# Delta-rule chunks in a four-layer decoder trunk: VectorE's order of work, and the next chunk's spreading placed ahead of the state's write

## Chip, cores and metric

The kernel runs on one core of a Trainium2 chip. The metric is the time of one execution on the device, in microseconds (us), as the median of several runs. A profiled execution gives a trace of every engine beside it.

## What is computed

The whole kernel is one inference step of a four-layer decoder trunk (sparse attention, gated delta rule, RG-LRU, sparse attention, each followed by a convolutional feed-forward layer) for one prompt of 512 tokens and eight sample tokens. The change lies in the second layer's delta rule over the prompt. In the reference it reads, cut to what matters (the reference takes chunks of 64 tokens, the kernel chunks of 128; the result is the same function):

```python
gcum = jnp.cumsum(gc, axis=-1)
decay = jnp.exp(jnp.where(incl, gcum[..., :, None] - gcum[..., None, :], NEG))
kb = kc * bc[..., None]
lower = jnp.einsum('nbhid,nbhjd->nbhij', kb, kc) * decay * strict
A = lower + jnp.eye(C, dtype=jnp.float32)
rhs = jnp.concatenate([vc * bc[..., None], kb * jnp.exp(gcum)[..., None]], axis=-1)
sol = lax.linalg.triangular_solve(A, rhs, left_side=True, lower=True, unit_diagonal=True)
u_base, w_dec = sol[..., :DV], sol[..., DV:]
attn = jnp.einsum('nbhid,nbhjd->nbhij', qc, kc) * decay

def step(S, xs):
    q_i, k_i, ub, wd, at, g_i = xs
    u = ub - jnp.einsum('bhck,bhkv->bhcv', wd, S)
    o = jnp.einsum('bhck,bhkv->bhcv', q_i * jnp.exp(g_i)[..., None], S) + jnp.einsum('bhij,bhjv->bhiv', at, u)
    g_last = g_i[..., -1]
    S = S * jnp.exp(g_last)[..., None, None] + jnp.einsum(
        'bhck,bhcv->bhkv', k_i * jnp.exp(g_last[..., None] - g_i)[..., None], u)
    return S, o
```

## The kernel before

The trunk is a row of stages. Each is a block of its own, in which every engine has its own list of instructions and waits on counters of the others; the engines meet at a stage's end. The stage here is `gdn_chunks` (L1239 to L1515). It takes the 512 prompt tokens in four chunks of 128 (`NCH`, `CH`), eight heads of width 128, in two groups of four heads (`x` = 0, 1), everything in float32. Queries, keys and values lie in SBUF as feature by token, put there by the stage before; no weights are loaded, and the only DMA is the final state's write at the end (L1511).

The order of the work is written out by hand: for each engine one loop over chunks, in it a list of steps. Every step raises its engine's counter of its group by one (`then_inc`), and `after(engine, who, x, step, c)` waits until `who` has done that step of chunk `c` for group `x`; with `None` for the step it waits for everything of the chunk before. The names of the steps stand in `pe_steps`, `act_steps` and `dve_steps` (L1246 to L1253). PSUM's eight banks are four for each group, numbers 0 to 3.

One chunk goes as follows:

- Spreading (TensorE, `products`, L1294): `spread_g` and `spread_b` copy each head's row of accumulated log decay and of beta to all 128 partitions. Then the products `qk` (queries by keys) and `kk` (keys by `k_beta`, L1328 and L1329).
- ScalarE makes `exp_g` and, from VectorE's `decay` differences (L1446), their exponential.
- VectorE makes `k_beta`, `v_beta`, `q_exp`, `k_exp`, `attn`, and the matrix `lower_t`, in two parts by partitions (L1458 and the line behind it), masked by `strict`. All VectorE operations through the helper `tt` carry line L1430, and most of ScalarE's carry L1393.
- The inversion of the triangular matrix. TensorE turns `lower_t` (`turn_l`, matmuls with the identity, L1313 and L1336), ScalarE copies it to `lower` (L1405). On blocks of 16, three rounds square `power` and `power_t` and grow the inverse `inv_t` (L1306); VectorE adds each growth to `inv_t`. Then three joins (`pair`, `turn`, `join`) take the blocks from 16 to 32, 64 and 128, with `mask0` and `mask1` made by VectorE ahead of the first; the result is `full_t`.
- TensorE turns `v_beta` (`turn_v`, L1299), applies the state (`k_state`), VectorE subtracts (`rhs`), TensorE solves, ScalarE copies `u`. Then for each group `out` (L1383, L1384) and `update`, the product of `k_left` and `u`.
- VectorE copies the output to `v.y` (L1500, seen in the trace as `all_xn_t_sb`), scales the state by its last decay (`decay_s`) and adds `update` (`add_s`).

At the head of a chunk TensorE waits for all of the chunk before:

```python
after(pe, "dve", x, None, c)
after(pe, "act", x, None, c)
```

## Time and profile before

| | us |
|---|---|
| median of 3 runs | 3374.48 |
| lowest and highest | 3372.79, 3377.38 |
| the profiled execution's own time | 3377.42 |
| its span in the trace | 3375.8 |
| mean granted TensorE clock | 0.954 of full |
| stage of the chunks in the trace | about 1134 to 1331 |

The span is the time from the first instruction to the last in the trace, which the profiled execution's own time exceeds by 1.6 us. Times in the rows are microseconds from the span's start. PE is TensorE's matmuls and PEld its weight loads, DVE is VectorE, ACT is ScalarE. A float32 matmul shows as two records where it is a product, and as one where it is a transpose (L1299). The clock is a share of 2.4 GHz, so 0.50 is 1.2 GHz.

### The profile page before, as it was taken

What the parts mean: (1) busy time and instruction counts of PE and PEld (TensorE: products, weight loads), DVE (VectorE), ACT (ScalarE), POOL (GpSimd) and SP (SyncE); (2) the same over time, 40 slices, a digit from 0 to 9 for tenths busy, and PEclk for the clock granted to TensorE, in tenths of its full rate; (3) what the DMA queues carried; (4) which work ended last, traced back from release to release, by engine and by line L of the source; (5) the groups of instructions that cost most, each with busy time, mean ns of one, the idle gap of its engine ahead of it and who ended that gap; (6) DMA issues with size and microseconds to landing.
All of it is one profiled execution on the core that took longest, in us unless ns stands there. A gap on an engine that the chain in (4) does not pass through costs nothing. (4 is left out here: it accounts for less than half of the span.)

```text
span 3375.8 us, 73291 instructions
## 1 busy us (share of the span) xinstructions
PE 3055.0 (90%) x30538; PEld 2845.3 (84%) x30538; DVE 1840.4 (55%) x3293; ACT 1281.6 (38%) x2267; POOL 80.5 (2%) x142
## 2 busy tenths in 40 slices
PE   5988889999899788689999888999979889989998
PEld 5975579999899778479999888999979855889997
DVE  3346646646567554456546565654633456566364
ACT  2236534324255322124233493433322255444242
POOL 0002100000000000000000000000000021000000
PEclk9989999999999898689999998999989999999999
DMA  6635314222322001214222322322265453142322
GB/s 189 200 110 167 113 32 168 81 94 74 87 82 82 6 2 58 81 62 150 88 99 73 98 76 70 142 83 100 80 138 190 145 162 109 32 143 90 110 78 78
DMA packets 154543, 339.44 MB, mean 101 GB/s; under 512 B 58884, under 2 KB 93316, under 8 KB 141332
## 3 DMA queue, kind: packets, MB, share of 16 engines
q1 hardware_dynamic: 145300, 296.04, 27.5%
q0 software_dynamic: 7424, 37.76, 3.2%
q8 instruction: 211, 3.46, 0.4%
q10 hardware_dynamic: 1536, 1.60, 0.2%
q14 instruction: 72, 0.59, 0.1%
HBM read 318.40 MB, written 32.12 MB: 104 GB/s over the span
## 5 line engine op out<-in xcount | busy, mean ns | idle before, releaser
L471 PE MATMUL ffn_ps<-ffn_x_hi_sb,ffn_w_hi_sb 128*128 128x260 f32 x2816 | 571.3, 284 | 49.0 <-DVE ffn_w_lo_sb L592 45.8
L471 PE MATMUL ffn_ps<-ffn_x_hi_sb,ffn_w_lo_sb 128*128 128x260 f32 x2816 | 570.3, 284 | 0.0
L471 PE MATMUL ffn_ps<-ffn_x_lo_sb,ffn_w_hi_sb 128*128 128x260 f32 x2816 | 569.9, 284 | 0.0
L471 PEld LDWEIGHTS ffn_ps<-ffn_x_hi_sb,ffn_w_hi_sb 128*128 128x128 f32 x2816 | 437.7, 190 | 51.4 <-DVE ffn_w_lo_sb L592 47.5
L471 PEld LDWEIGHTS ffn_ps<-ffn_x_hi_sb,ffn_w_lo_sb 128*128 128x128 f32 x2816 | 437.3, 190 | 0.0
L471 PEld LDWEIGHTS ffn_ps<-ffn_x_lo_sb,ffn_w_hi_sb 128*128 128x128 f32 x2816 | 436.7, 190 | 0.0
L526 ACT ACTIVATE ffn_w_hi_sb<-ffn_raw_sb 128x2048 fp32r<-128x2048 f32 (+2 forms) x148 | 249.4, 1685 | 338.5 <-PE ffn_ps L471 338.5
L549 ACT ACTIVATE ffn_pre_sb<-ffn_ps 128x520 f32<-128x520 f32 x176 | 106.6, 606 | 600.7 <-PE ffn_ps L471 312.8
L586 DVE TENSOR_TENSOR ffn_w_lo_sb<-ffn_raw_sb,ffn_w_hi_sb 128x2048 fp32r<-128x2048 f32 (+2 forms) x148 | 296.1, 2001 | 44.9 <-ACT ffn_w_hi_sb L526 44.9
L607 DVE SCALAR_TENSOR_TENSOR ffn_conv_sb<-ffn_pre_sb,ffn_conv_w_sb,ffn_conv_sb 128x512 f32<-128x512 f32 x176 | 132.3, 752 | 340.8 <-ACT ffn_conv_sb L551 340.8
L471 PE MATMUL ffn_ps<-ffn_inner_hi_sb,ffn_w_hi_sb 128*128 128x260 f32 x1408 | 284.7, 283 | 6.5 <-DVE ffn_inner_lo_sb L625 3.4
L471 PE MATMUL ffn_ps<-ffn_inner_lo_sb,ffn_w_hi_sb 128*128 128x260 f32 x1408 | 283.8, 283 | 0.0
L471 PE MATMUL ffn_ps<-ffn_inner_hi_sb,ffn_w_lo_sb 128*128 128x260 f32 x1408 | 282.9, 282 | 0.0
L471 PEld LDWEIGHTS ffn_ps<-ffn_inner_hi_sb,ffn_w_hi_sb 128*128 128x128 f32 x1408 | 217.1, 188 | 9.2 <-DVE ffn_w_lo_sb L586 4.8
L471 PEld LDWEIGHTS ffn_ps<-ffn_inner_hi_sb,ffn_w_lo_sb 128*128 128x128 f32 x1408 | 216.9, 188 | 0.0
L471 PEld LDWEIGHTS ffn_ps<-ffn_inner_lo_sb,ffn_w_hi_sb 128*128 128x128 f32 x1408 | 216.7, 188 | 0.0
L645 DVE TENSOR_TENSOR all_x_t_sb<-all_x_t_sb,ffn_ps 128x520 f32<-128x520 f32 x64 | 44.5, 696 | 268.1 <-PE ffn_ps L471 268.1
L2716 DVE TENSOR_REDUCE nsat_nmax_sb<-nsat_ps 128x2 f32<-128x256 f32 (+3 forms) x128 | 104.9, 821 | 125.0 <-PE nsat_ps L2493 124.9
L201 PE MATMUL nsab_ps<-nsab_x_hi_sb,nsab_w_hi_sb 128*128 128x260 f32 x512 | 114.0, 305 | 43.9 <-DVE nsab_w_lo_sb L291 22.7
L2504 PE MATMUL nsat_ps<-all_consts_sb,nsat_prob_sb 128*128 128x128 f32 x640 | 109.5, 290 | 45.4 <-DVE nsat_prob_t_sb L2741 23.9
L2644 ACT ACTIVATE nsat_prob_t_sb<-nsat_ps 128x128 f32<-128x128 f32 (+3 forms) x192 | 82.2, 437 | 160.0 <-PE nsat_ps L2504 159.8
L2635 ACT ACTIVATE nsat_prob_sb<-nsat_ps,nsat_nmax_sb 128x128 f32<-128x128 f32 (+3 forms) x256 | 132.7, 525 | 25.9 <-DVE nsat_nmax_sb L2716 24.2
(484 smaller groups left out, 5798.7 us busy)
## 6 DMA issues: line engine op xcount, KB each, us to landing
ffn_raw_sb<-ffn_w_in SPq DMA_DIRECT2D x84, 1024.0 KB, 4.8
ffn_raw_sb<-ffn_w_out SPq DMA_DIRECT2D x32, 768.0 KB, 4.2
nsa_ring_sb<-sel_pages SPq DMA_DIRECT2D x160, 128.0 KB, 2.5
ffn_raw_sb<-ffn_w_out SPq DMA_DIRECT2D x32, 640.0 KB, 4.0
...
```

The source lines that it names most:

```text
L201: mm = pe.matmul(out(h), w, x[:, h * H:(h + 1) * H], start=start and k == 0, stop=stop and k == 2)
L471: mm = pe.matmul(psf[:, bank + h, 0:H], wp[:, w[0], w[1]:w[1] + P], xp[:, h * H:(h + 1) * H], start=start and k == 0, stop=stop and k == 2)
L526: act.activation(w_hi[:, s, 0:size], raw[:, s, 0:size], ACT.Copy).then_inc(hi_done, 1)
L549: act.activation(pre[:, s, vg, 2:2 + N].rearrange("p (h n) -> p h n", h=2), src, ACT.Copy)
L586: dve.tensor_tensor(w_lo[:, s, 0:size], raw[:, s, 0:size], w_hi[:, s, 0:size], ALU.subtract).then_inc(lo_done, 1)
L607: own.did(dve.scalar_tensor_tensor(y[:, 0:T], x[:, 1:1 + T], w[1], y[:, 0:T], ALU.mult, ALU.add))
L645: dve.tensor_tensor(x, x, psf[:, 2 * (m % 3):2 * (m % 3) + 2, 0:H], ALU.add).then_inc(added, 1)
L2504: mm = pe.transpose(ps[:, 4 + g2, kt * P:(kt + 1) * P], prob[:, s % 4, g2, kt * P:(kt + 1) * P], g.ident)
L2635: act.activation(prob[:, s % 4, g2, 0:(i + 1) * P], ps[:, 2 * (s % 2) + g2, 0:(i + 1) * P], ACT.Exp, bias=nmax[:, s % 4, g2:g2 + 1], accum ...
L2644: act.activation(prob_t[:, s % 4, g2, 0:(i + 1) * P], ps[:, 4 + g2, 0:(i + 1) * P], ACT.Copy).then_inc(copied[g2], 1)
L2716: dve.tensor_reduce(nmax[:, s % 4, :], ps[:, 2 * (s % 2):2 * (s % 2) + 2, 0:(i + 1) * P], AX, ALU.max, negate=True).then_inc(maxed, 1)
```

## The change

Four things, all inside `gdn_chunks`:

1. VectorE's order. After `k_beta` and `decay` of both groups come `lower_t` and `strict` group by group, then `power_t` and `inv_t`, then `v_beta` and `power`, and the masks directly behind. `q_exp`, `k_exp` and `attn` stand behind the first, second and third pair of adds to `inv_t`.
2. TensorE's order. `kk` follows the spreading, `qk` stands behind `turn_l` and waits for ScalarE's `lower` of its group (its PSUM bank is the turning's). The banks are dealt anew: `spread_b` in 2, `kk` in 1, `qk` in 0. `pair0` waits for the third add (`grown2`), since the masks are earlier.
3. The head of a chunk. TensorE waits for `k_left` and `u` of the chunk before, no longer for all of it, so the spreading may run ahead of `decay_s` and `add_s`. ScalarE's `exp_g` waits for `decay_s`, which still reads the old one.
4. The output's copy to `v.y` goes from VectorE to ScalarE (`store_o`), as its last step in a chunk; the turning of the next chunk's `lower_t`, which writes the same bank, waits for it.

The diff, cut to these:

```diff
@@ TensorE
                 for x in range(2):
-                    after(pe, "dve", x, None, c)
-                    after(pe, "act", x, None, c)
+                    if c:
+                        after(pe, "dve", x, "k_left", c - 1)
+                        after(pe, "act", x, "u", c - 1)
                     products(x, 0, lambda j: v.spread[:, 4 * x + j, :], lambda j: v.rows[:, cols])
-                    products(x, 1, lambda j: v.spread[:, GH + 4 * x + j, :], lambda j: v.rows[:, cols])
-                for x in range(2):
-                    products(x, 3, lambda j: v.k[:, 4 * x + j, cols], lambda j: v.q[:, 4 * x + j, cols])
+                    products(x, 2, lambda j: v.spread[:, GH + 4 * x + j, :], lambda j: v.rows[:, cols])
                 for x in range(2):
                     after(pe, "dve", x, "k_beta", c)
...
                 for x in range(2):
                     after(pe, "dve", x, "strict", c)
+                    if c:
+                        after(pe, "act", x, "store_o", c - 1)
                     half_turns(x, 0, buf["lower_t"], (low, high))
...
+                for x in range(2):
+                    after(pe, "act", x, "lower", c)
+                    products(x, 0, lambda j: v.k[:, 4 * x + j, cols], lambda j: v.q[:, 4 * x + j, cols])
...
-                        after(pe, "dve", x, "masks" if m == 0 else "joined0", c)
+                        after(pe, "dve", x, "grown2" if m == 0 else "joined0", c)
...
                 for x in range(2):
+                    after(pe, "dve", x, "attn", c)
                     turns(x, 0, lambda j: buf["v_beta"][:, x, j, :])
@@ ScalarE
                 for x in range(2):
-                    after(act, "dve", x, None, c)
+                    if c:
+                        after(act, "dve", x, "decay_s", c - 1)
                     after(act, "pe", x, "spread_g", c)
                     run(x, buf["exp_g"][:, x], ps[:, x, 0], ACT.Exp)
...
+                for x in range(2):
+                    after(act, "pe", x, "out", c)
+                    run(x, chunk(v.y, x, c), ps[:, x, 3])
@@ VectorE
                     after(dve, "pe", x, "spread_b", c)
-                    tt(x, buf["k_beta"][:, x], chunk(v.k, x, c), ps[:, x, 1])
-                    tt(x, buf["v_beta"][:, x], chunk(v.v, x, c), ps[:, x, 1])
+                    tt(x, buf["k_beta"][:, x], chunk(v.k, x, c), ps[:, x, 2])
...
                 for x in range(2):
-                    tt(x, buf["q_exp"][:, x], chunk(v.q, x, c), buf["exp_g"][:, x])
-                    after(dve, "dve", x, "k_beta", c)
-                    tt(x, buf["k_exp"][:, x], buf["k_beta"][:, x], buf["exp_g"][:, x])
-                for x in range(2):
                     after(dve, "act", x, "exp_decay", c)
-                    after(dve, "pe", x, "qk", c)
-                    tt(x, buf["attn"][:, x], ps[:, x, 3], buf["decay"][:, x])
                     after(dve, "pe", x, "kk", c)
...
                 for x in range(2):
+                    tt(x, buf["v_beta"][:, x], chunk(v.v, x, c), ps[:, x, 2])
                     after(dve, "act", x, "lower", c)
...
                 for e in range(3):
                     for x in range(2):
                         after(dve, "pe", x, f"grow{e}", c)
                         tt(x, buf["inv_t"][:, x], buf["inv_t"][:, x], ps[:, x, 1, :, low], ALU.add)
...
+                    for x in range(2):
+                        if e == 0:
+                            tt(x, buf["q_exp"][:, x], chunk(v.q, x, c), buf["exp_g"][:, x])
+                        elif e == 1:
+                            tt(x, buf["k_exp"][:, x], buf["k_beta"][:, x], buf["exp_g"][:, x])
+                        else:
+                            after(dve, "pe", x, "qk", c)
+                            tt(x, buf["attn"][:, x], ps[:, x, 0], buf["decay"][:, x])
...
                     after(dve, "pe", x, "out", c)
-                    dve.tensor_copy(chunk(v.y, x, c), ps[:, x, 3]).then_inc(dve_did[x], 1)
                     tt(x, state[:, x], state[:, x], wide(buf["exp_g"][:, x, :, CH - 1:CH]))
```

How the instructions stand at three places of the second chunk. The first is VectorE, from its second `decay` on (`x2` is two such instructions, one for each group of heads). Before:

```order
L1430 TENSOR_TENSOR gdnc_q_exp_sb<-gdn_q_sb,gdnc_exp_g_sb 128x512
L1430 TENSOR_TENSOR gdnc_k_exp_sb<-gdnc_k_beta_sb,gdnc_exp_g_sb 128x512
L1430 TENSOR_TENSOR gdnc_q_exp_sb<-gdn_q_sb,gdnc_exp_g_sb 128x512
L1430 TENSOR_TENSOR gdnc_k_exp_sb<-gdnc_k_beta_sb,gdnc_exp_g_sb 128x512
L1430 TENSOR_TENSOR gdnc_attn_sb<-gdnc_ps,gdnc_decay_sb 128x512
L1458 TENSOR_TENSOR gdnc_lower_t_sb<-gdnc_ps,gdnc_decay_sb 64x4x64
L1430 TENSOR_TENSOR gdnc_lower_t_sb<-gdnc_ps,gdnc_decay_sb 64x512
L1430 TENSOR_TENSOR gdnc_attn_sb<-gdnc_ps,gdnc_decay_sb 128x512
L1458 TENSOR_TENSOR gdnc_lower_t_sb<-gdnc_ps,gdnc_decay_sb 64x4x64
L1430 TENSOR_TENSOR gdnc_lower_t_sb<-gdnc_ps,gdnc_decay_sb 64x512
L1430 TENSOR_TENSOR gdnc_lower_t_sb<-gdnc_lower_t_sb,gdnc_strict_t_packed_sb 128x4x64 x2
L1465 SCALAR_TENSOR_TENSOR gdnc_power_t_sb<-gdnc_lower_t_sb,gdnc_same_packed_sb 128x256 x2
```

Now, from the first `decay`:

```order
L1453 SCALAR_TENSOR_TENSOR gdnc_decay_sb<-gdnc_ps,gdn_cum_tok_sb,all_consts_sb 128x128 x4
L1438 TENSOR_TENSOR gdnc_k_beta_sb<-gdn_k_sb,gdnc_ps 128x512
L1453 SCALAR_TENSOR_TENSOR gdnc_decay_sb<-gdnc_ps,gdn_cum_tok_sb,all_consts_sb 128x128 x4
L1459 TENSOR_TENSOR gdnc_lower_t_sb<-gdnc_ps,gdnc_decay_sb 64x4x64
L1438 TENSOR_TENSOR gdnc_lower_t_sb<-gdnc_ps,gdnc_decay_sb 64x512
L1438 TENSOR_TENSOR gdnc_lower_t_sb<-gdnc_lower_t_sb,gdnc_strict_t_packed_sb 128x4x64
L1459 TENSOR_TENSOR gdnc_lower_t_sb<-gdnc_ps,gdnc_decay_sb 64x4x64
L1438 TENSOR_TENSOR gdnc_lower_t_sb<-gdnc_ps,gdnc_decay_sb 64x512
L1438 TENSOR_TENSOR gdnc_lower_t_sb<-gdnc_lower_t_sb,gdnc_strict_t_packed_sb 128x4x64
L1465 SCALAR_TENSOR_TENSOR gdnc_power_t_sb<-gdnc_lower_t_sb,gdnc_same_packed_sb 128x256 x2
L1438 TENSOR_TENSOR gdnc_inv_t_sb<-gdnc_power_t_sb,gdnc_ident_packed_sb 128x256 x2
L1438 TENSOR_TENSOR gdnc_v_beta_sb<-gdn_v_sb,gdnc_ps 128x512
```

The five wide rows of 128x512 ahead of `lower_t`, and the one between its parts, are gone; `strict` (the rows that read `strict_t_packed`) stands at the end of each group's three, and the first `v_beta` behind `inv_t`.

The second place is VectorE in the rounds of the inversion. Before, from `power` to the masks' first rows:

```order
L1472 SCALAR_TENSOR_TENSOR gdnc_power_sb<-gdnc_lower_sb,gdnc_same_packed_sb 128x256 x2
L1430 TENSOR_TENSOR gdnc_inv_t_sb<-gdnc_inv_t_sb,gdnc_ps 128x256 x6
L1479 TENSOR_TENSOR gdnc_mask_sb<-gdnc_lower_sb,gdnc_pair_packed_sb 128x256
L1430 TENSOR_TENSOR gdnc_mask_sb<-gdnc_lower_sb,gdnc_pair_packed_sb 128x256
L1479 TENSOR_TENSOR gdnc_mask_sb<-gdnc_lower_sb,gdnc_pair_packed_sb 128x256
```

Now, from the last mask to the first join:

```order
L1438 TENSOR_TENSOR gdnc_mask_sb<-gdnc_lower_sb,gdnc_pair_packed_sb 128x256
L1438 TENSOR_TENSOR gdnc_inv_t_sb<-gdnc_inv_t_sb,gdnc_ps 128x256 x2
L1438 TENSOR_TENSOR gdnc_q_exp_sb<-gdn_q_sb,gdnc_exp_g_sb 128x512 x2
L1438 TENSOR_TENSOR gdnc_inv_t_sb<-gdnc_inv_t_sb,gdnc_ps 128x256 x2
L1438 TENSOR_TENSOR gdnc_k_exp_sb<-gdnc_k_beta_sb,gdnc_exp_g_sb 128x512 x2
L1438 TENSOR_TENSOR gdnc_inv_t_sb<-gdnc_inv_t_sb,gdnc_ps 128x256 x2
L1438 TENSOR_TENSOR gdnc_attn_sb<-gdnc_ps,gdnc_decay_sb 128x512 x2
L1438 TENSOR_TENSOR gdnc_inv_t_sb<-gdnc_inv_t_sb,gdnc_ps 128x256 x2
```

The six adds stood together, with the masks behind; now the masks come first, and `q_exp`, `k_exp` and `attn` stand behind a pair of adds each.

The third place is TensorE, from the spreading on (in the first chunk, as in all). Before:

```order
L1294 MATMUL gdnc_ps<-gdn_rows_sb,gdn_spread_sb 128x128 x16
L1294 MATMUL gdnc_ps<-gdn_q_sb,gdn_k_sb 128x128 x8
L1328 MATMUL gdnc_ps<-gdnc_k_beta_sb,gdn_k_sb 64x128
L1329 MATMUL gdnc_ps<-gdnc_k_beta_sb,gdn_k_sb 64x64
L1328 MATMUL gdnc_ps<-gdnc_k_beta_sb,gdn_k_sb 64x128
```

Now, from the last product of `kk` to the first squarings:

```order
L1327 MATMUL gdnc_ps<-gdnc_k_beta_sb,gdn_k_sb 64x64
L1312 MATMUL gdnc_ps<-all_consts_sb,gdnc_lower_t_sb 64x64 x8
L1336 MATMUL gdnc_ps<-all_consts_sb,gdnc_lower_t_sb 64x64 x4
L1312 MATMUL gdnc_ps<-all_consts_sb,gdnc_lower_t_sb 64x64 x8
L1336 MATMUL gdnc_ps<-all_consts_sb,gdnc_lower_t_sb 64x64 x4
L1293 MATMUL gdnc_ps<-gdn_q_sb,gdn_k_sb 128x128 x8
L1305 MATMUL gdnc_ps<-gdnc_power_sb,gdnc_power_t_sb 64x64 x8
L1305 MATMUL gdnc_ps<-gdnc_power_t_sb,gdnc_power_sb 64x64 x8
```

The eight products of queries by keys stood between spreading and `kk`; now they stand behind the turning of `lower_t` and directly ahead of the first squaring.

## Rows read from the trace of the kernel before

**Rows 1.** The page: busy time, share of the span and instructions of each engine
```profile
PE 3055.0 (90%) x30538; PEld 2845.3 (84%) x30538; DVE 1840.4 (55%) x3293; ACT 1281.6 (38%) x2267; POOL 80.5 (2%) x142
```

**Rows 2.** Windows, second chunk: us, busy us (instructions) per engine, PEclk, DMA share, GB/s
```profile
1183.00:1233.00 50.00, 41.63 (x735) 39.72 (x735) 27.57 (x59) 14.17 (x34) 0.00 (x0) 0.93 0.01 2
```

**Rows 3.** Timeline, PE, second chunk: start, us, engine, line, x records [idle before <-releaser]
```profile
1185.85 3.84 PE L1294 MATMUL gdnc_ps<-gdn_rows_sb,gdn_spread_sb 128*128 128x128 f32 x32 [1.09 <-DVE gdnc_state_sb L1430]
1189.53 1.95 PE L1294 MATMUL gdnc_ps<-gdn_q_sb,gdn_k_sb 128*128 128x128 f32 x16
...
1198.79 0.80 PE L1313 MATMUL gdnc_ps<-all_consts_sb,gdnc_lower_t_sb 64*64 64x64 f32 x10 [5.43 <-DVE gdnc_lower_t_sb L1430]
...
1201.72 1.12 PE L1306 MATMUL gdnc_ps<-gdnc_power_sb,gdnc_power_t_sb 64*64 64x64 f32 x16 [0.34 <-DVE gdnc_power_sb L1472]
...
1206.40 0.63 PE L1306 MATMUL gdnc_ps<-gdnc_power_sb,gdnc_power_t_sb 64*64 64x64 f32 x16
...
1209.43 1.10 PE L1306 MATMUL gdnc_ps<-gdnc_power_sb,gdnc_power_t_sb 64*64 64x64 f32 x32
...
1212.89 0.68 PE L1306 MATMUL gdnc_ps<-gdnc_inv_t_sb,gdnc_mask_sb 64*64 64x64 f32 x16 [1.20 <-DVE gdnc_mask_sb L1430]
...
1232.22 1.06 PE L1294 MATMUL gdnc_ps<-gdnc_u_sb,gdnc_k_left_sb 128*128 128x128 f32 x8
1234.36 1.83 PE L1294 MATMUL gdnc_ps<-gdn_rows_sb,gdn_spread_sb 128*128 128x128 f32 x14 [1.09 <-DVE gdnc_state_sb L1430]
```

**Rows 4.** Timeline, DVE, second chunk, same columns
```profile
1187.94 0.69 DVE L1430 TENSOR_TENSOR gdnc_k_beta_sb<-gdn_k_sb,gdnc_ps 128x512 f32<-128x512 f32 x1 [1.55 <-PE gdnc_ps L1294]
...
1191.37 1.12 DVE L1446 SCALAR_TENSOR_TENSOR gdnc_decay_sb<-gdnc_ps,gdn_cum_tok_sb,all_consts_sb 128x128 f32<-128x128 f32 x4
1192.41 0.68 DVE L1430 TENSOR_TENSOR gdnc_q_exp_sb<-gdn_q_sb,gdnc_exp_g_sb 128x512 f32<-128x512 f32 x1
...
1195.53 0.43 DVE L1458 TENSOR_TENSOR gdnc_lower_t_sb<-gdnc_ps,gdnc_decay_sb 64x256 f32<-64x256 f32 x1
1195.97 0.68 DVE L1430 TENSOR_TENSOR gdnc_lower_t_sb<-gdnc_ps,gdnc_decay_sb 64x512 f32<-64x512 f32 x1
...
1198.33 0.74 DVE L1430 TENSOR_TENSOR gdnc_lower_t_sb<-gdnc_lower_t_sb,gdnc_strict_t_packed_sb 128x256 f32<-128x256 f32 x2
1199.00 0.75 DVE L1465 SCALAR_TENSOR_TENSOR gdnc_power_t_sb<-gdnc_lower_t_sb,gdnc_same_packed_sb 128x256 f32<-128x256 f32 x2
...
1201.24 0.43 DVE L1472 SCALAR_TENSOR_TENSOR gdnc_power_sb<-gdnc_lower_sb,gdnc_same_packed_sb 128x256 f32<-128x256 f32 x1 [0.82 <-ACT gdnc_lower_sb L1393]
...
1208.94 0.42 DVE L1430 TENSOR_TENSOR gdnc_inv_t_sb<-gdnc_inv_t_sb,gdnc_ps 128x256 f32<-128x256 f32 x1 [1.91 <-PE gdnc_ps L1306]
...
1211.27 0.89 DVE L1430 TENSOR_TENSOR gdnc_inv_t_sb<-gdnc_inv_t_sb,gdnc_ps 128x256 f32<-128x256 f32 x2 [1.21 <-PE gdnc_ps L1306]
```

**Rows 5.** Timeline, ACT, second chunk
```profile
1187.11 0.60 ACT L1393 ACTIVATE gdnc_exp_g_sb<-gdnc_ps 128x512 f32<-128x512 f32 x1 [7.51 <-PE gdnc_ps L1294]
...
1200.43 0.38 ACT L1405 ACTIVATE gdnc_lower_sb<-gdnc_ps 128x256 f32<-128x256 f32 x1 [7.28 <-PE gdnc_ps L1336]
```

**Rows 6.** Windows of 0.5 us, PE: us, busy (instructions), PEclk, DMA share, GB/s
```profile
1198.50:1199.00 0.50, 0.21 (x4) 0.61 0.00 0
...
1205.00:1205.50 0.50, 0.50 (x16) 0.56 0.00 0
```

**Rows 7.** Timeline, PE, first chunk
```profile
1134.67 6.64 PE L1294 MATMUL gdnc_ps<-gdn_rows_sb,gdn_spread_sb 128*128 128x128 f32 x32 [6.07 <-DVE gdnc_state_sb L1436]
...
1149.97 0.80 PE L1313 MATMUL gdnc_ps<-all_consts_sb,gdnc_lower_t_sb 64*64 64x64 f32 x10 [4.98 <-DVE gdnc_lower_t_sb L1430]
...
1152.90 1.12 PE L1306 MATMUL gdnc_ps<-gdnc_power_sb,gdnc_power_t_sb 64*64 64x64 f32 x16 [0.34 <-DVE gdnc_power_sb L1472]
...
1157.89 0.63 PE L1306 MATMUL gdnc_ps<-gdnc_power_sb,gdnc_power_t_sb 64*64 64x64 f32 x16
```

**Rows 8.** Timeline, DVE, first chunk: its second k_beta
```profile
1141.35 0.69 DVE L1430 TENSOR_TENSOR gdnc_k_beta_sb<-gdn_k_sb,gdnc_ps 128x512 f32<-128x512 f32 x1 [0.47 <-PE gdnc_ps L1294]
```

More of the change, by code:

```diff
@@ L1249, in gdn_chunks @@
     act_steps = ["exp_g", "exp_decay", "lower", "power0", "power_t0", "power1", "power_t1", "power2", "paired0", "inv0",
[L1250 to L1253 removed]
+                 "paired1", "inv1", "paired2", "inv2", "v_tok", "u", "store_o"]
+    dve_steps = ["k_beta", "decay", "lower_t", "strict", "power_t", "inv_t", "v_beta", "power", "masks", "grown0", "q_exp",
+                 "grown1", "k_exp", "grown2", "attn", "joined0", "joined1", "joined2", "rhs", "k_left", "decay_s", "add_s"]
     with ExitStack() as ctx:
```

21 lines of the change are left out of this document (8 added, 13 removed).

## Prediction, made before the changed kernel was run

> **What bounds the kernel now.** A difference under 0.2% (some 7 us) can't be told from no change in a measurement of this kernel, so the question is what the 200 us of the delta-rule chunks can give. I read four views. The page first [rows 1]: over the whole span TensorE is busy 90% and VectorE 55%, which says matmuls bound the kernel; but that is an average over stages of which this change touches one. The windows over that stage next [rows 2]: in a chunk of about 48.5 us (spreading starts at 1185.85 and again at 1234.36) TensorE is busy 41.6 of 50 us, at a mean clock of 0.93. Then the timeline of TensorE in the second chunk [rows 3], for the places where it stands still: 5.43 us before the turning of `lower_t`, 1.20 before `pair0`, 1.09 before the next chunk's spreading. Last the timelines of VectorE and ScalarE beside it [rows 4, 5], for what it waits on.
>
> The largest wait is VectorE's. From the first `k_beta` at 1187.94 it works without a pause past the second `inv_t` at about 1200.4; what the matrix needs of that (`k_beta`, `decay`, `lower_t`, `strict`) is mixed with `v_beta`, `q_exp`, `k_exp` and `attn`, eight wide operations at 0.6 us each (the five from 1192.41 to 1195.53 take 3.12) [rows 4]. TensorE has finished its products at 1193.36 (1198.79 less 5.43) and waits for `strict`. And it pays twice: its granted clock falls from full (2.4 GHz) to half (1.2 GHz) at the end of that wait and comes back in the half microsecond after 1205 [rows 6]. So the first squaring round goes at half: it lasts from 1201.72 to 1206.40, 4.68 us, where the same instructions in the second round, 1206.40 to 1209.43, need 3.03 [rows 3].
>
> **The change, part by part.** Times below are from the start of a chunk's spreading (1185.85 in the second), at full clock.
>
> *Triangular matrix first.* The spreading ends at 3.84 [rows 3]. `k_beta` of the first half of the heads starts at 2.09 as before and its `decay` at 2.70. The second `k_beta` waits for the spreading: 3.88. Its `decay` follows at 4.49 and takes 1.04 (1192.41 less 1191.37), to 5.53. Now `lower_t` comes at once: 5.60, its second part 0.44 later (1195.53 to 1195.97), 6.04. `strict` of the same half must wait for it, 0.71 more: 6.75. In the rows TensorE starts 0.46 after `strict` (1198.33 to 1198.79), so the turning starts at **7.21 in place of 12.94**. The products `kk`, now ahead of `qk`, need 1.95 from 3.84 on and are done at 5.8, before that. The other half's `strict` is 1.50 later (0.35 + 0.44 + 0.71), its turning at 8.71.
>
> *What then ends last.* `power` is made by VectorE after two `power_t`, two `inv_t` (0.34 each) and the first `v_beta` (0.60): 8.25 + 0.33 + 1.34 + 0.60 = 10.5; with 0.48 from VectorE's start to TensorE's (1201.24 to 1201.72) the squaring could start at 11.0. But TensorE has `qk` ahead of it, and half of that now waits for ScalarE's `lower` of the second half: turning issued from 8.71, 24 of the 64-column records at 0.032 us (96 in 3.03), 0.25 to land, 0.81 for the two copies (1200.43 to 1201.24), so 10.5; its 16 records, half of 32 in 3.68 us, take 0.92. Squaring starts at **11.4 in place of 15.87**: 4.47 us less, in three chunks 13.4. In the first chunk the clock is at half during the spreading, which takes 6.64 [rows 7], and stays so: second `k_beta` 1141.35 [rows 8], `strict` 2.87 later, turning at 1144.68, squaring 4.19 after that, 1148.87 in place of 1152.90: 4.0.
>
> *The clock.* The one wait of over 5 us is cut to about 1.4 us (5.8 to 7.2), then come bursts with gaps of 0.8 us or less. The waits of 1.09 and 1.20 us are followed by no fall: a mean clock of 0.93 over 50 us is what the one stretch of 6.8 us at half makes by itself (0.5 x 6.8 / 50 = 0.07) [rows 2, 3]. The change's own is not in the trace: it is longer than these, and the stretch after it is thin. The ends are no fall (the round saves 1.65 us in three chunks and 1.96 in the first, 4.99 less 3.03 [rows 7]) and a fall in every chunk (saves nothing, and turning and `qk` at half cost 0.5 + 1.8 us more). I stand near the first, since 1.4 is nearer to 1.2 than to 5.4, but take off a third of one fall, 0.3 x (1.65 + 2.3) = 1.2 us. Sum here: 4.95 + 1.96 - 1.2 = 5.7.
>
> *Masks before the adds.* `pair0` waits for `mask` today; then it waits for the third add, 1211.27 + 0.48 = 1211.75 in place of 1212.89: 1.14 in each of four chunks, 4.6. The masks go to VectorE's wait for the first `grow`.
>
> *Wide operations in gaps.* Two at 0.60 go behind each pair of adds. What covers them are VectorE's waits for TensorE: 1.91 us before the second round's adds, 1.21 before the third's [rows 4]. `q_exp` fits in the one, `k_exp`, 1.2 us, just into the other: cost 0 to 0.1. `attn`, 1.2 us, takes the place in which the four masks stand now, 1.3 us (0.34 each). I cost all three at nothing; without cover it would be up to 0.6 x 6 us a chunk.
>
> *Spreading ahead of the state's write.* TensorE no longer waits for `add_s`, but for `k_left` and `u`, both long done. `update` is issued at 1232.22 and takes 0.9: spreading from 1233.12 in place of 1234.36, 1.24 us at three joints, 3.7. The next `k_beta` comes 2.09 later, when VectorE has finished both `add_s` (half a microsecond before), so the gain arrives.
>
> *Copy of the result to ScalarE.* On VectorE an operation of 128x512 takes 0.69 us, 0.6 to the next [rows 4]; on ScalarE an operation of that shape takes 0.60 [rows 5] and its next task is `exp_g`, 1.26 us after the spreading starts: free. The copy held `decay_s` and `add_s` behind it, which counts only at the stage's end, 0.6. The added waits of the turning and of `exp_g` for ScalarE's copy or for `decay_s` are over before they are reached. No DMA moves.
>
> Sum: 13.4 + 4.0 + 5.7 + 4.6 + 3.7 + 0.6 = **32 us** of the profiled execution's 3377.4, so 3345.4. That execution lies at the top of the three runs; their median is 3374.5, and against it the forecast is **3342.5 us**.
>
> **The rivals.** *The clock falls all the same.* For it: between 5.8 and 8.7 TensorE has only one burst of 0.7 us. Then the 5.7 us of the clock's sum are gone, and turning and `qk` at half cost up to 2.3 us in each of four chunks: 32 - 5.7 - 9.2 = 17, **3357**. Against it: such bursts follow at less than a microsecond. The Trainium skill's page "TensorE: Matmul & The Clock Gate", Part 4, states that transposes in transpose mode do not count as activity for the clock; by that rule, were it to hold for the turning of `lower_t`, the stretch would look idle until `qk` and this rival would be the case. In this trace the turnings of `lower_t` are plain matmuls with the identity.
>
> *VectorE sets the pace inside the inversion.* If the wide operations are not covered, each of six delays an add by up to 0.6 us: 14.4 in four chunks, **3357** too. Against it: the waits in rows 4 are as long as what is put there.
>
> *Slower.* TensorE never gets back to full clock, since the chunk now has many gaps and no long dense stretch ahead of the squaring. Rows 3 and 7 give the price: spreading takes 6.64 us at half in place of 3.84; with 41.6 busy us a chunk, nearly all at full today, that is some 30 us a chunk, less 33 in all: **about 3460**. It is level with today where some 80 us of the stage more than now go at half (each microsecond at half loses 1 - 3.84/6.64 = 0.42). Against it: in the second half of the chunk, which doesn't change, the clock came back in every chunk.
>
> *It does not do what it says.* If the engines' waits kept the old order in effect, nothing would move, **3374**. The order of instructions shows the new one on both engines.
>
> **How the numbers follow.** Forecast 0.76; clock 0.12; VectorE 0.07; no effect 0.03; slower 0.02. The range goes down to 3336 (no fall, the first of the runs of before 1.7 us under their median, a little more at the joints) and up to 3354, which takes in one or two falls, half-covered wide operations, and the better part of both middle rivals. Faster by over 0.2% are the first three, 0.95; within it 0.03; slower 0.02.
>
> **What the profile after would show.** Right: a wait before the turning of about 1.4 us, and 7.2 us from spreading to turning; squaring at 11.4; PEclk near 1.00 in the second to fourth chunk; `pair0` behind an `inv_t` add, not a mask; chunks of about 39.7 us; spreading directly behind `update`. Wrong would be: PEclk at half around the first round; VectorE without a pause between the rounds and TensorE waiting for adds; a new wait of over 2 us anywhere on TensorE.

## The result and the profile after

| | before | after |
|---|---|---|
| median of 4 runs each, us | 3374.65 | **3348.05** |
| lowest and highest | 3372.79, 3377.38 | 3346.9, 3351.53 |
| ratio, with its 95% interval | | 0.9922 (0.9908 to 0.9937) |
| profiled execution's own time | 3377.42 | 3347.42 |
| span in the trace | 3375.8 | 3345.8 |
| stage of the chunks: first spreading to next stage's first matmul | 200.13 | 174.86 |

The change is faster by 26.6 us of medians; 32 were forecast. The time lies inside the range (3336 to 3354), 5.5 us over the forecast.

The page after, line for line with [rows 1]: TensorE's busy time is lower by 5 us while the span is lower by 30, so what went is mostly waiting of TensorE.

```profile
PE 3049.6 (91%) x30538; PEld 2843.0 (85%) x30538; DVE 1836.0 (55%) x3285; ACT 1285.7 (38%) x2275; POOL 80.3 (2%) x142
```

The windows of after, one for each chunk from its first spreading to the next one's, the last to its `update` (columns as in [rows 2]):

```profile
1132.71:1177.38 44.67, 42.10 (x720) 40.18 (x721) 24.69 (x55) 15.25 (x36) 0.00 (x0) 0.90 0.01 2
1177.38:1219.17 41.79, 39.22 (x722) 37.25 (x721) 25.88 (x58) 15.36 (x36) 0.00 (x0) 0.96 0.01 2
1219.17:1259.53 40.36, 37.79 (x723) 35.87 (x721) 25.89 (x58) 15.36 (x36) 0.00 (x0) 1.00 0.01 3
1259.53:1302.00 42.47, 39.89 (x716) 37.82 (x715) 25.19 (x55) 14.76 (x35) 0.00 (x0) 0.92 0.01 3
```

The second and third chunk hold the same instructions, but take 41.79 and 40.36 us. The seventh number of the line, PEclk, says why: 0.96 in the one, 1.00 in the other, 0.92 in the fourth. The clock was to be near 1.00 in all three.

TensorE's timeline after, second chunk, answers to [rows 3]:

```profile
1177.38 3.74 PE L1293 MATMUL gdnc_ps<-gdn_rows_sb,gdn_spread_sb 128*128 128x128 f32 x32
...
1184.55 0.51 PE L1312 MATMUL gdnc_ps<-all_consts_sb,gdnc_lower_t_sb 64*64 64x64 f32 x10 [1.54 <-DVE gdnc_lower_t_sb L1438]
...
1186.16 0.80 PE L1312 MATMUL gdnc_ps<-all_consts_sb,gdnc_lower_t_sb 64*64 64x64 f32 x10 [0.64 <-DVE gdnc_lower_t_sb L1438]
...
1187.69 2.90 PE L1293 MATMUL gdnc_ps<-gdn_q_sb,gdn_k_sb 128*128 128x128 f32 x16
1190.52 0.68 PE L1305 MATMUL gdnc_ps<-gdnc_power_sb,gdnc_power_t_sb 64*64 64x64 f32 x16
...
1193.60 0.63 PE L1305 MATMUL gdnc_ps<-gdnc_power_sb,gdnc_power_t_sb 64*64 64x64 f32 x16
...
1198.95 0.68 PE L1305 MATMUL gdnc_ps<-gdnc_inv_t_sb,gdnc_mask_sb 64*64 64x64 f32 x16
```

The spreading has no wait in brackets any more. The wait of 5.43 us is now 1.54 with a second one of 0.64, and the turning starts at 7.17 (1184.55 less 1177.38). `pair0` at the end has no wait either, and the first round lasts 3.08 us (1190.52 to 1193.60) where it lasted 4.68. But the second half's turning reads 0.80 for its ten records, not 0.51, and `qk` 2.90. The third chunk has both at full clock:

```profile
1226.34 0.51 PE L1312 MATMUL gdnc_ps<-all_consts_sb,gdnc_lower_t_sb 64*64 64x64 f32 x10 [1.54 <-DVE gdnc_lower_t_sb L1438]
...
1227.96 0.51 PE L1312 MATMUL gdnc_ps<-all_consts_sb,gdnc_lower_t_sb 64*64 64x64 f32 x10 [0.64 <-DVE gdnc_lower_t_sb L1438]
...
1228.86 2.09 PE L1293 MATMUL gdnc_ps<-gdn_q_sb,gdn_k_sb 128*128 128x128 f32 x16
1230.88 0.68 PE L1305 MATMUL gdnc_ps<-gdnc_power_sb,gdnc_power_t_sb 64*64 64x64 f32 x16
```

There the squaring starts at 11.71 (1230.88 less 1219.17), in the second at 13.14. Half-microsecond windows of the second chunk, TensorE alone (us, busy and instructions, PEclk), show the fall as [rows 6] do for before:

```profile
1185.50:1186.00 0.50, 0.02 (x1) 1.00 0.00 0
1186.00:1186.50 0.50, 0.34 (x6) 0.58 0.00 0
...
1189.00:1189.50 0.50, 0.50 (x4) 0.51 0.00 0
1189.50:1190.00 0.50, 0.50 (x7) 1.00 0.00 0
```

The clock drops to half (1.2 GHz) at about 1186.1, at the end of the second wait, and is back by 1189.5, before the squaring. All chunks side by side, in us from each chunk's first spreading:

| | turning | squaring | second round | `pair0` | chunk |
|---|---|---|---|---|---|
| before, chunks 1, 2, 3, 4 | 15.30, 12.94, 12.95, 12.94 | 18.23, 15.87, 15.87, 15.88 | 23.22, 20.55, 20.30, 20.08 | 29.71, 27.04, 26.79, 26.57 | 51.18, 48.51, 48.26, 52.18 |
| after, chunks 1, 2, 3, 4 | 9.92, 7.17, 7.17, 7.16 | 16.02, 13.14, 11.71, 14.02 | 19.10, 16.22, 14.78, 17.67 | 24.45, 21.57, 20.14, 23.02 | 44.67, 41.79, 40.36, 48.04 |

(The fourth runs to the next stage's first matmul.) Three of four chunks had a fall between the turning and the squaring, and chunk 3 had none.

VectorE's timeline after, same chunk, for the operations that were moved into gaps [rows 4]:

```profile
1194.15 1.29 DVE L1438 TENSOR_TENSOR gdnc_q_exp_sb<-gdn_q_sb,gdnc_exp_g_sb 128x512 f32<-128x512 f32 x2
1196.15 0.42 DVE L1438 TENSOR_TENSOR gdnc_inv_t_sb<-gdnc_inv_t_sb,gdnc_ps 128x256 f32<-128x256 f32 x1 [0.71 <-PE gdnc_ps L1305]
1196.85 0.42 DVE L1438 TENSOR_TENSOR gdnc_inv_t_sb<-gdnc_inv_t_sb,gdnc_ps 128x256 f32<-128x256 f32 x1 [0.28 <-PE gdnc_ps L1305]
1197.18 1.28 DVE L1438 TENSOR_TENSOR gdnc_k_exp_sb<-gdnc_k_beta_sb,gdnc_exp_g_sb 128x512 f32<-128x512 f32 x2
1198.47 0.89 DVE L1438 TENSOR_TENSOR gdnc_inv_t_sb<-gdnc_inv_t_sb,gdnc_ps 128x256 f32<-128x256 f32 x2
```

`q_exp` is covered with 0.71 us to spare; `k_exp` ends just as the third adds are due (no wait before them), and `pair0` follows 0.48 after these.

### The profile page after: what moved, and what is told of

It is laid out like the page before. It is cut to its first block and busy times, and to the rows that moved or that the text cites. A ratio compares the mean times of both kernels' runs of the same rounds, so it can differ in the third digit from the quotient of the medians.

```text
span 3345.8 us, 73297 instructions
## 1 busy us (share of the span) xinstructions
PE 3049.6 (91%) x30538; PEld 2843.0 (85%) x30538; DVE 1836.0 (55%) x3285; ACT 1285.7 (38%) x2275; POOL 80.3 (2%) x142
```

## The experiments

The theory going in: the parts give what the sum says at full clock, and the shortfall is the clock, which falls at the waits of 1.54 and 0.64 us. The rival: TensorE's clock is incidental and VectorE's new order costs more than written. Twelve runs followed, in four groups on four chips, each beside runs of the kernel before; ratios are to those (0.9922 is after's own). Each was traced in one execution, and what is said of chunks and stages is read from that one.

### after_again: the same kernel once more

> The changed kernel once more. Clock theory: a chunk whose TensorE clock stays full from spreading to the first squaring takes 40.3 us (as the third chunk did), one with a fall between turning and squaring 41.8 to 43.2; which chunks fall differs from one execution to the next, so the time scatters by some 4 us around 3348. Rival (VectorE or ScalarE makes the difference between chunks): the same chunks are long again, with a full clock in at least one of the long ones.

Measured: 3348.58 us (3347.29 to 3351.28), ratio 0.9922 (0.9908 to 0.9935), stage 175.09. The squarings start at 16.14, 13.18, 11.71 and 14.03: falls in the same three chunks. The expectation was wrong in that point: which chunks fall did not differ between the two traced executions. The rival (the same chunks long, with a full clock) is excluded too, since the clock is at half in the long ones.

### fill_products and fill_turns: is it the waits that make the clock fall?

fill_products puts products whose result nobody reads into the two waits, six into the first and two into the second:

```diff
+                for x, n in ((0, 4), (1, 2)):
+                    if c:
+                        after(pe, "act", x, "store_o", c - 1)
+                    for j in range(n):
+                        pe.matmul(ps[:, x, 3, j, :], v.k[:, 4 * x + j, cols], v.q[:, 4 * x + j, cols], start=True, stop=True)
                 for x in range(2):
                     after(pe, "dve", x, "strict", c)
...
                     mm.then_inc(pe_did[x], 1)
+                    if x == 0:
+                        for j in range(2):
+                            pe.matmul(ps[:, 1, 3, j, :], v.k[:, 4 + j, cols], v.q[:, 4 + j, cols], start=True, stop=True)
```

> Adds 6 products of keys by queries into an unused bank in the wait before the turning of lower_t and 2 in the wait between the two turnings, 1.8 us of TensorE work a chunk whose result nobody reads. Clock theory: the clock stays full in the second to fourth chunk, squaring starts 11.7 us after the spreading in each, chunks of 40.3 us, and the kernel takes about 3342 to 3343. Rival (the falls have another cause, and the added work only stands in the way): 3348 to 3352, with falls as before.

fill_turns puts 12 and 4 transposes in transpose mode there instead, also unread:

```diff
+                for x, n in ((0, 4), (1, 4)):
...
+                    for j in range(n):
+                        pe.transpose(ps[:, x, 3, j, :], v.k[:, 4 * x + j, cols], g.ident)
+                    for j in range(4):
+                        pe.transpose(ps[:, x, 3, j, :], v.q[:, 4 * x + j, cols], g.ident) if x else None
...
+                    if x == 0:
+                        for j in range(4):
+                            pe.transpose(ps[:, 1, 3, j, :], v.k[:, 4 + j, cols], g.ident)
```

> The same two waits filled with 12 and 4 transposes in transpose mode of keys or queries in place of the products, also 1.8 us a chunk, result unused. If such transposes hold the clock up as products do: full clock and 3342 to 3343. If they don't count for the clock, as the Trainium skill's page 'TensorE: Matmul & The Clock Gate', Part 4, says: falls in about the same number of chunks as the changed kernel, or more, 3347 to 3352.

Measured: fill_products 3337.56 us (3334.78 to 3342.51), ratio 0.9884 (0.9869 to 0.9899), stage 169.01; fill_turns 3337.08 (3336.17 to 3344.31), 0.9891 (0.9875 to 0.9906), stage 169.09. First the windows of the second and third chunk of fill_products:

```profile
1177.17:1217.54 40.37, 39.96 (x739) 37.80 (x738) 25.90 (x57) 15.36 (x36) 0.00 (x0) 1.00 0.01 2
1217.54:1257.91 40.37, 39.96 (x738) 37.80 (x737) 25.89 (x57) 15.36 (x36) 0.00 (x0) 1.00 0.01 2
```

then the same of fill_turns:

```profile
1179.70:1220.07 40.37, 39.83 (x738) 37.58 (x737) 25.90 (x57) 15.36 (x36) 0.00 (x0) 1.00 0.01 2
1220.07:1260.44 40.37, 39.83 (x738) 37.58 (x737) 25.89 (x58) 15.36 (x36) 0.00 (x0) 1.00 0.01 2
```

and TensorE in the third chunk of fill_turns, between `kk` and `qk`:

```profile
1225.63 1.09 PE L1334 MATMUL gdnc_ps<-all_consts_sb,gdn_k_sb 128*128 128x128 f32 x8
1226.56 0.60 PE L1336 MATMUL gdnc_ps<-all_consts_sb,gdn_q_sb 128*128 128x128 f32 x4
1227.24 0.51 PE L1312 MATMUL gdnc_ps<-all_consts_sb,gdnc_lower_t_sb 64*64 64x64 f32 x10
```

Both chunks are what chunk 3 of after is, 40.37 us, at PEclk 1.00; the turning still starts at 7.17, the squaring at 11.71 in chunks 2 to 4, and in the first at 14.44 and 14.52. TensorE has more work, and the stage is 5.9 us shorter; both kernels are also some 5 us faster than was expected, of which more below.

Since chunk 3 of after did not fall with its waits empty, a chunk without a fall could be luck of its place in time. The first chunk excludes that. In the five kernels of the rows below the clock of the first chunk comes back from half 5.5 to 5.8 us after the spreading starts, and the turnings start 9.9 to 10.0 and 11.5 to 11.6 us after it. Here is the stretch from 12.8 to 15.8 us behind it (TensorE's busy time, instructions, PEclk), in the order after, after_no_ahead (a run below, in which these waits are as empty as in after), fill_products, fill_turns, k_turned_early (below; only the first wait filled):

```profile
1145.51:1148.51 3.00, 3.00 (x16) 0.50 0.00 0
1148.93:1151.93 3.00, 3.00 (x15) 0.50 0.00 0
1146.87:1149.87 3.00, 3.00 (x61) 1.00 0.00 0
1149.32:1152.32 3.00, 3.00 (x59) 1.00 0.00 0
1145.66:1148.66 3.00, 3.00 (x62) 1.00 0.00 0
```

With the waits empty the first chunk fell in all three executions (after_again is the third), and in none of the four with filling (k_turned_again is the fourth). So the falls come from those waits, and cost 1.6, 1.4 and 2.9 us in chunks 1, 2 and 4. VectorE's order is the same with and without the filling, so the rival is excluded. The two fills differ by 0.1 us of stage: transposes in transpose mode held the clock as products did. The Trainium skill's page "TensorE: Matmul & The Clock Gate", Part 4 (PE-mode transpose), says that the full clock does not engage for transpose mode, which does not count as busy in the same way. This trace does not agree, as far as it goes: on this float32 kernel a clock that was full stayed full through them. Whether transposes by themselves would bring it back from half no run shows.

### before_fill and before_fill22: what did the fall of before cost?

The same filling in the wait of 5.43 us of the kernel before, again unread. The first of the two carries 40 products, though its expectation speaks of 22; the second has the 22:

```diff
                 for x in range(2):
+                    after(pe, "dve", x, "decay", c)
+                    for j in range(11):
+                        pe.matmul(ps[:, x, 0, j % 4, :], v.k[:, 4 * x + j % 4, cols], v.q[:, 4 * x + j % 4, cols], start=True, stop=True)
+                for x in range(2):
                     after(pe, "dve", x, "strict", c)
```

> The kernel before, with 22 products of keys by queries (4.9 us a chunk, result unused) in TensorE's wait of 5.4 us ahead of the turning of lower_t; nothing else changed. Clock theory: no fall at that wait; turning to squaring 2.4 us in place of 2.93, first round 3.07 in place of 4.2 to 5.0, so some 2 us a chunk: stage about 192 us, kernel 3366 to 3368. Rival (the falls cost nothing there, since VectorE sets the pace): 3375.

> The kernel before with 22 products (4.9 us a chunk, result unused) in its wait of 5.4 us ahead of the turning; the run before_fill had 40 in it (9 us), so its turning came 3.6 us late. Clock theory: turning at 12.9 to 13.0 us after the spreading as before, from there to squaring 2.3 (was 2.93), first round 3.08 (was 4.2 to 5.0): some 2.1 us a chunk, stage about 192 us, kernel 3366. Rival: 3375, nothing gained since the copy by ScalarE or VectorE's power sets the pace.

Measured: before_fill 3380.24 us (3377.57 to 3384.75), ratio 1.002 (1.0011 to 1.0029), stage 206.63: 40 products last 9.0 us, so the turning starts at 16.58 and the kernel is slower: a filling longer than the wait costs its excess. Its first rounds took 3.08 us in all four chunks, so the clock was full there too. before_fill22: 3364.0 (3361.11 to 3365.99), 0.9969 (0.9957 to 0.9981), stage 191.56. Windows of its second and third chunk, then TensorE in the third:

```profile
1183.27:1229.54 46.27, 42.60 (x764) 40.56 (x764) 26.97 (x59) 14.18 (x34) 0.00 (x0) 1.00 0.01 2
1229.54:1275.82 46.28, 42.60 (x764) 40.56 (x764) 26.99 (x59) 14.18 (x34) 0.00 (x0) 1.00 0.01 2
```

```profile
1236.99 5.18 PE L1335 MATMUL gdnc_ps<-gdn_q_sb,gdn_k_sb 128*128 128x128 f32 x44
...
1242.48 0.51 PE L1313 MATMUL gdnc_ps<-all_consts_sb,gdnc_lower_t_sb 64*64 64x64 f32 x10 [0.32 <-DVE gdnc_lower_t_sb L1434]
```

The turning starts at 12.94 as in before; a chunk takes 46.28 in place of 48.51, 2.2 us less. So 8.6 us of the stage (200.13 less 191.56) were the clock alone, to be had with none of the old work moved; the other 22.5 of the 31.1 us from before to fill_products came by moving.

### masks_only, ahead_only, after_no_ahead: single parts

masks_only is before with the four masks ahead of the adds (the names of the steps and the wait; the mask instructions move with them):

```diff
-                 "power", "grown0", "grown1", "grown2", "masks", "joined0", "joined1", "joined2",
+                 "power", "masks", "grown0", "grown1", "grown2", "joined0", "joined1", "joined2",
...
-                        after(pe, "dve", x, "masks" if m == 0 else "joined0", c)
+                        after(pe, "dve", x, "grown2" if m == 0 else "joined0", c)
```

> The kernel before, with only the masks ahead of the adds and pair0 waiting for the third add. Theory: second round to pair0 5.35 us in place of 6.49 in each chunk, 4.6 us in all, about 3371. Rival (the masks delay the first add, or pair0 then waits for something else): 3375.

Measured: 3366.95 us (3363.62 to 3373.28), ratio 0.9983 (0.9974 to 0.9992), stage 197.19. From the second round to `pair0` 5.35 us, as in after, in place of 6.49: 1.14, the forecast to the hundredth. TensorE's timeline of its second chunk, where the wait of 1.20 us stood [rows 3]:

```profile
1206.50 1.10 PE L1306 MATMUL gdnc_ps<-gdnc_power_sb,gdnc_power_t_sb 64*64 64x64 f32 x32
1207.62 1.15 PE L1306 MATMUL gdnc_ps<-gdnc_inv_t_sb,gdnc_power_sb 64*64 64x64 f32 x32
1208.82 0.68 PE L1306 MATMUL gdnc_ps<-gdnc_inv_t_sb,gdnc_mask_sb 64*64 64x64 f32 x16
```

The stage gained 2.9, not 4.6. The first rounds took 4.92, 5.00, 5.03 and 5.05 us (from the squaring's first row to the second round's), where before had 4.99, 4.68, 4.43 and 4.20: the clock came back later in them (20.6 us after the spreading in the second chunk, where it was 19.6), which took 1.7 back. The kernel's time fell by 8.1 us against the runs beside it; the rest beyond the stage's 2.9 lies in stages that this edit doesn't touch (see the rest of the program below).

ahead_only is before with the banks, waits and ScalarE copy of the new joint:

```diff
                 for x in range(2):
-                    after(pe, "dve", x, None, c)
-                    after(pe, "act", x, None, c)
+                    if c:
+                        after(pe, "dve", x, "k_left", c - 1)
+                        after(pe, "act", x, "u", c - 1)
                     products(x, 0, lambda j: v.spread[:, 4 * x + j, :], lambda j: v.rows[:, cols])
```

> The kernel before with only the spreading ahead of the state's write and the output's copy on ScalarE. Theory: update to the next spreading 0.90 us in place of 2.14 at three joints, and 0.6 at the stage's end, 4.3 us in all: stage 195.8, kernel 3371. Rival (VectorE, not TensorE, sets the start of k_beta): the joint is shorter, but the turning comes later than 12.94 us after the spreading, by as much.

Measured: 3368.71 us (3362.3 to 3373.1), ratio 0.9982 (0.9973 to 0.9991), stage 195.1. Its joint on TensorE:

```profile
1230.61 1.06 PE L1294 MATMUL gdnc_ps<-gdnc_u_sb,gdnc_k_left_sb 128*128 128x128 f32 x8
1231.50 3.74 PE L1294 MATMUL gdnc_ps<-gdn_rows_sb,gdn_spread_sb 128*128 128x128 f32 x32
```

From `update` to the spreading 0.89 us in place of 2.14 [rows 3]: 1.25 a joint, as written. The turning starts 12.84 us after the spreading, no later than in before (12.94), which excludes the rival. after_no_ahead is after with the old wait back, and that alone:

```diff
                     if c:
-                        after(pe, "dve", x, "k_left", c - 1)
-                        after(pe, "act", x, "u", c - 1)
+                        after(pe, "dve", x, "add_s", c - 1)
```

> The changed kernel, with TensorE waiting at a chunk's head for the state's write of its group again. Theory: 1.24 us at three joints, 3.7 us slower than the changed kernel, 3352; a wait of about 1.1 us on TensorE is back ahead of each spreading, the final chunk as fast as in the changed kernel. Rival (the early start only made TensorE wait later, for VectorE's k_beta or at the turning): the same time as the changed kernel, 3348.

Measured: 3347.32 us (3344.99 to 3351.43), ratio 0.9916 (0.9902 to 0.9929): no slower than after. Its windows, first three chunks, and TensorE at the joint:

```profile
1136.13:1181.59 45.46, 42.39 (x721) 40.23 (x721) 25.37 (x56) 15.26 (x36) 0.00 (x0) 0.90 0.01 2
1181.59:1222.71 41.12, 38.04 (x721) 35.94 (x721) 25.90 (x57) 15.38 (x36) 0.00 (x0) 1.00 0.01 2
1222.71:1263.83 41.12, 38.04 (x721) 35.94 (x721) 25.90 (x57) 15.37 (x36) 0.00 (x0) 1.00 0.01 3
```

```profile
1222.71 3.50 PE L1293 MATMUL gdnc_ps<-gdn_rows_sb,gdn_spread_sb 128*128 128x128 f32 x29 [0.49 <-DVE gdnc_state_sb L1437]
```

The wait of 0.49 us is back, and a chunk at full clock takes 41.12 in place of 40.37: the early start is worth 0.75 us a joint, not 1.24, once ScalarE's copy of the result has let `add_s` start earlier (the wait for it was 1.09 with the copy on VectorE, and is 0.49 without). The time of the whole came out as the rival had it, but not for its reason: the chunks did get longer. Yet the stage is 172.95, 1.9 less than after's: only the first chunk fell here, which had cost after 4.3 us in chunks 2 and 4, more than three joints at 0.75. Whether a chunk falls does not hang on the lengths of its waits alone, which are the same (1.54 and 0.64) in chunks that fall and chunks that do not. That it hangs on where in time they lie is inferred: with each joint longer the later chunks lie elsewhere in time and none of them fell, while the first, which lies alike, fell in all three executions. On such a kernel the total time of a run with one part taken out does not give that part's worth; the offsets within a chunk do.

### wide_first: what the triangular matrix first is worth

fill_products with `q_exp` and `k_exp` back ahead of `lower_t`, and 16 unread products in place of six in the first wait, which is now longer, so that the clock holds:

```diff
                 for x in range(2):
+                    tt(x, buf["q_exp"][:, x], chunk(v.q, x, c), buf["exp_g"][:, x])
+                    after(dve, "dve", x, "k_beta", c)
+                    tt(x, buf["k_exp"][:, x], buf["k_beta"][:, x], buf["exp_g"][:, x])
+                for x in range(2):
                     after(dve, "act", x, "exp_decay", c)
```

> The changed kernel with the filling (16 products in the first wait, 2 in the second), and q_exp and k_exp of both groups back ahead of lower_t: VectorE's new order undone in part, at a clock that is held up. Theory: four operations at 0.60 us come back onto the path, turning at 9.6 us after the spreading in place of 7.17, chunks of 42.8 us in place of 40.37, stage 179, kernel about 3347. Rival (the order of VectorE is worth less than that, since TensorE's issue sets the pace once the clock is full): chunks of 40.4 to 41.5 us.

Measured: 3349.1 us (3347.89 to 3352.53), ratio 0.9923 (0.991 to 0.9937), stage 178.36. Its second chunk:

```profile
1176.87:1219.64 42.77, 42.19 (x759) 40.04 (x757) 25.90 (x58) 15.38 (x36) 0.00 (x0) 1.00 0.01 2
```

Four wide operations at 0.6 us ahead of the matrix: the turning 2.40 later (9.57), the chunk 2.40 longer, both at full clock. Each wide operation that stands ahead of `lower_t` costs its 0.6 us in full, and in the gaps of the rounds nothing. The longer filling is not what held the turning up: it waits for `strict` (0.18 us in this chunk).

### k_turned_early, k_turned_again, k_turned_fill: useful work in the wait

Instead of unread products, a real task: `turn_k` (the keys turned, until now behind `solve`) goes into the wait after `kk`. ScalarE copies it to a buffer, from which `k_left` is made.

```diff
+                    if c:
+                        after(pe, "act", x, "store_o", c - 1)
+                    turns(x, 3, lambda j: v.k[:, 4 * x + j, cols])
                 for x in range(2):
                     after(pe, "dve", x, "strict", c)
-                    if c:
-                        after(pe, "act", x, "store_o", c - 1)
+                    after(pe, "act", x, "k_tok", c)
...
-                    turns(x, 0, lambda j: v.k[:, 4 * x + j, cols])
...
+                    after(act, "pe", x, "turn_k", c)
+                    run(x, buf["k_tok"][:, x], ps[:, x, 3])
...
-                    after(dve, "pe", x, "turn_k", c)
-                    tt(x, buf["k_left"][:, x], ps[:, x, 0], wide(buf["decay"][:, x, :, CH - 1:CH]))
+                    after(dve, "act", x, "k_tok", c)
+                    tt(x, buf["k_left"][:, x], buf["k_tok"][:, x], wide(buf["decay"][:, x, :, CH - 1:CH]))
```

> The changed kernel, with the turning of the keys (turn_k, 0.43 us for each group) moved from between the solves into the wait after kk, ScalarE copying it to SBUF. Theory: the tail of a chunk is TensorE's issue, so turn_v to the end of update gets 0.87 us shorter, a chunk without a fall takes 39.5 us, and the wait before the turning of lower_t is half filled, so fewer falls: stage 166 to 171, kernel 3334 to 3344. Rivals: the solve of the second group then waits for rhs (no gain in the tail, 3345 to 3348); or ScalarE's two copies delay its decay and with it strict (turning later than 7.3 us after the spreading).

k_turned_again is the same kernel once more; k_turned_fill adds six unread products behind the turned keys.

> The kernel with the keys turned early once more, to see whether its full clock was luck. If the 0.87 us of turnings in the wait are enough to hold the clock: no fall between kk and the second round in any chunk, chunks of 39.7 us, stage 166.4, kernel 3334 to 3338. If it was luck: a fall in one chunk or more, that chunk 41 to 42.5 us, stage 168 to 172, kernel up to 3342.

> The same with 6 products (1.3 us, result unused) behind it, ahead of the turning. Theory: turning may start up to 0.7 us late in the first group (k_turned and filling together are 2.2 us in a wait of 1.5), but the clock stays full in all chunks: 39.5 to 40.0 us a chunk, stage about 167, kernel about 3335. Rival: as slow as the changed kernel with filling alone (3337.5) or slower, since the filling now stands in the way.

Measured: k_turned_early 3336.24 us (3334.09 to 3337.76), ratio 0.9892 (0.9877 to 0.9907), stage 166.42; k_turned_again 3338.63 (3338.3 to 3338.93), 0.9891 (0.9875 to 0.9908), stage 166.41; k_turned_fill 3340.91 (3340.27 to 3342.17), 0.9905 (0.989 to 0.992), stage 168.56. Windows of k_turned_early, then TensorE in its third chunk:

```profile
1175.33:1215.05 39.72, 38.45 (x723) 35.88 (x722) 25.71 (x57) 16.44 (x38) 0.00 (x0) 1.00 0.01 2
1215.05:1254.76 39.71, 38.44 (x722) 35.87 (x721) 25.71 (x57) 16.44 (x38) 0.00 (x0) 1.00 0.01 3
```

```profile
1219.73 0.66 PE L1298 MATMUL gdnc_ps<-all_consts_sb,gdn_k_sb 128*128 128x128 f32 x4
...
1221.34 0.66 PE L1298 MATMUL gdnc_ps<-all_consts_sb,gdn_k_sb 128*128 128x128 f32 x4
...
1222.22 0.51 PE L1312 MATMUL gdnc_ps<-all_consts_sb,gdnc_lower_t_sb 64*64 64x64 f32 x10 [0.23 <-DVE gdnc_lower_t_sb L1441]
```

The first wait is 0.23 us, no chunk fell in either profile, and a chunk takes 39.71: 0.65 less than the 40.37 of a filled one, because the tail from the first row of `turn_v` to that of the second `update` is 9.19 us in place of 9.84. 0.87 were forecast; the other 0.22 went to what the expectation named as a rival: the second group's solve now waits for `rhs` (its first record starts 0.23 us after the one before, where they follow at 0.11). By its stage this is the shortest version (166.4 us against 169.0 of the filled ones). By the kernel's time it is faster than after by 0.3% and than before by 1.1%, and is not to be told from the filled ones, whose ratios are 0.9884 and 0.9891. Their first chunks did not fall either, where all three executions with empty waits did, so the full clock was not luck. The second wait (0.65) was still empty: filling the first was enough. The six products more stand in the way, as that run's rival had it: turning at 7.77, chunk 40.24, and there was no fall left for them to prevent.

## Why the prediction was right, and where it was off

Each step by the numbers of the chunk without a fall, or of the filled kernels:

| step | forecast | measured |
|---|---|---|
| turning starts (chunks 2 to 4) | 7.21 | 7.17 |
| turning starts, first chunk | 10.01 | 9.92 |
| wait before the turning | 1.4 | 1.54, then 0.64 |
| squaring starts, clock held | 11.4 | 11.71 |
| first round | 3.03 | 3.08 |
| masks, a chunk | 1.14 | 1.14 |
| joint, update to spreading | 1.24 | 1.25 with ScalarE's copy; by TensorE's earlier start alone 0.75 |
| wide operations in gaps | 0 to 0.1 | 0; covered |
| falls of the clock | a third of one, 1.2 | three, 5.9 |
| sum of the stage | 32.0 | 25.3 |

The mechanism was as written, step by step, and the time lies in the range for that reason. *The term that was mis-sized is the allowance for the clock.* The prediction put the wait of about 1.4 us nearer to the 1.09 and 1.20 us that are followed by no fall than to the 5.43 that is, and took off a third of one fall. It named what spoke against that (the thin stretch after it), and left it at that weight. A fall came in three chunks of four. The two waits do not stand alone: 1.54 us, then a burst of 0.97, then 0.64. The waits of before that no fall follows, ahead of `pair0` and of the spreading, are single ones. That the pair is what matters, and not the 1.54 by itself, was not tested. One fall cost 1.4 to 2.9 us; 2.3 had been written for the turning and `qk` at half, and the first round was spared in chunks 1 and 2, as the clock was back before it. In chunk 4 the half clock lasted from 1268.0 to 1274.8, into the round (3.65 us in place of 3.08).

*The remaining 2.1 us* are small sizes. With the clock held the stage gains 31.1 (200.13 less 169.01), against 33.2 for the sum without the allowance. Squaring starts 0.3 later, 1.2 in four chunks: the second turning starts at 8.79 for 8.71, its 24 records went out in 0.90 us (1227.96 to 1228.86), where 0.032 a record, taken from the squaring, made 0.77, and all of `qk` takes 2.02 behind that (to 1230.88). Its first half went out from 9.69 to 10.68, and the second, forecast for 10.5, stood behind it. And the first round of before was taken as 4.68 us in all chunks, from the second; in the third and fourth it was 4.43 and 4.20, which left 0.7 less to gain. The rounds' 3.08 for 3.03 make the last 0.2.

*Readings that were wrong without moving the sum.* The half of `qk` that takes 0.92 us is 8 records (`qk` has 16 in all, [rows 3]), not 16. And the first chunk's clock does not stay at half: it is back 5.9 us after the spreading starts (PEclk 0.92 from 1140.5 to 1141.0 in before) and falls again at 12.7. So more than half a microsecond of the spreading's 6.64 ran at full clock, and the price of the slower case, taken from 6.64 to 3.84, is too low.

*The rivals.* The first, the clock falls all the same (3357), was half right: 5.9 of its 15 us came. The prediction had named for it what the Trainium skill's page "TensorE: Matmul & The Clock Gate", Part 4, says of transpose mode. The falls came although the turnings of `lower_t` are plain matmuls, and transposes in the waits prevented them, so that was not the reason. VectorE did not set the pace: it waits 0.71 us before the second round's adds, and the third's pushed nothing back. TensorE got back to full clock in every chunk, which excludes the slower case.

*Against the measured median*: the forecast gain was 32.0, the stage's is 25.3, the medians differ by 26.6. The rest of the program scatters, though its code is the same: from the next stage's first matmul to the span's end it took 2041.0 us in before, 2038.2 in after, 2037.7 in fill_products, 2030.6 in fill_turns, 2033.1 and 2034.4 in the two runs of the turned keys, 2033.0 in masks_only, 2040.9 in wide_first. So the fills' medians are 10.5 and 11.0 us under after's where their stage accounts for 5.9. The rest follows for the most part from TensorE's clock further on: summed over the trace's record of the granted clock, it stood at half for 201 us of those 2041.0 in before, 192 in after, 198 in fill_products, 193 in masks_only and 177 in fill_turns, and over all fourteen traces the rest is the longer, the longer its clock is at half (correlation 0.87). Whether the stage's end sets that off, or it differs from one execution to the next by itself, was not tested; a gain of a few microseconds in the total is no measure of a change in this stage.
